# The first feed-forward product of a two-block kernel on one NeuronCore: two plain column blocks by token halves in four PSUM banks, the second block's weights split early

## The chip, the cores and the metric

The kernel runs on one NeuronCore of a Trainium2 chip. TensorE (PE) multiplies into PSUM, eight banks of 2 KB per partition; VectorE (DVE) and ScalarE (ACT) do elementwise work on SBUF and PSUM, GpSimd (POOL) on SBUF alone; SyncE (SP) and POOL issue the DMAs. Every engine works through its own instructions in the order in which they were written, and waits on semaphores. The metric is the device time of one execution in microseconds (us); lower is better.

## The reference

The program is two transformer-like blocks over 512 tokens of width 1024, in float32. The change lies at the end of the second block (D = 1024, D_FF = 4096), cut here to what matters:

```python
h = layer_norm(DEEPNORM_ALPHA * h + m @ w_out[l], ln1_g[l], ln1_b[l])
f = jnp.square(jax.nn.relu(h @ w_ff1[l])) @ w_ff2[l]
h = layer_norm(DEEPNORM_ALPHA * h + f, ln2_g[l], ln2_b[l])
```

## The kernel before, in words

**Products.** Every large product splits both operands into a high part (`fp32r`, an ACT copy: `split`, `up_hi_of`, `left_hi`, `right_hi`) and the rest (a DVE subtraction: `lower`), and issues three matmuls for each 128-row step: high x high, high x low, low x high (`three`, lines 456 to 458).

**Blocks.** `block_list` cuts the weights into blocks of 1 MB, numbered n. SP loads block n into `RAW[n % 2]`, ACT writes `WH`, DVE writes `WL`; there are two such pairs of slots and a third one (`WH[2]`, `WL[2]`), used by the two blocks of `OWN`, whose lower part POOL computes (`split_own`). DVE works for n: `split(n + 1)`, `side(n)`, `stage(n)` and `drain(n)`; ACT likewise. `W_OUT2` has four blocks, WO2 to WO2+3: the first two give columns 0 to 511 of `m @ w_out` (`tm_block`), the last two columns 512 to 1023 (`tm_pair`), each in banks 2 to 5, one bank for each 128-token tile. `stage` splits the left operand for the pair (ACT `x_hi`, DVE `x_lo`), and `drain(WO2+1)` adds the first two blocks' banks to the residual (`add_half`, four instructions on line 1765), which frees banks 2 to 5 for the pair.

**The layer norm rows.** The pair finishes one token tile after another. For each tile DVE adds (line 1765), takes statistics, centres (1788) and scales (1797), with a reciprocal root on POOL between; then PE transposes the row (`turn_row`, eight 128x128 transposes into banks 6 and 7, line 567), ACT writes the high part `TH` (line 1169) and a plain copy `H1T` (line 1170), and DVE subtracts into `TL` (`h1_rows_lo`). Rows 0 and 1 are turned within the pair, rows 2 and 3 within the next product.

**The first feed-forward product.** `h @ w_ff1` has 4096 columns in eight groups of 512. Group 0 is computed plainly, as two blocks of 256 columns (`ff1_0`, `ff1_0 + 1`), each in banks 0 and 1. The first goes through `fm_block_by_halves`: all of its work for tokens 0 to 255, during which rows 2 and 3 are turned, and then that for tokens 256 to 511, with 256-wide matmuls. The second goes through `fm_block` with 512-wide matmuls; it uses the same banks 0 and 1, so it waits until ACT has taken the first block out of them (`relus(0)`, line 1222). Its weights are loaded into `RAW[1]` and split after the rows.

**Groups 1 to 7** are computed by Winograd's form of Strassen's scheme, seven products a group (`ff1_multiply(q, i)`, order P1, P5, P6, P2, P7, P3, P4; 24 matmuls, 256 wide, in each; g counts them from 0 to 48). It wants sums of quadrants of `h` (`left_sums`, `left_sum_hi`, `left_sum_lo`), sums of quadrants of the weights (`up_sums`), and five rotating slots of split weights (`UPH`, `UPL`). Banks are combined by `part_copy` on ACT and `add_part` on DVE (line 1972): P6 waits for the copy of P1, P4 waits for `add_part` of P7. `difference` (1978) is work for the next product.

**The turn.** `ff @ w_ff2` follows in the same scheme: 28 products p of 24 matmuls, 512 wide. SP loads or POOL adds (an accumulating DMA) 1 MB of weights for each into one of four buffers `MRAW`, ACT makes `right_hi(p)` and `left_hi(p)`, DVE `right_lo(p)` and `left_lo(p)`, in three slots. The first of these stand among the last products of the first half, written out by hand in the loops `for g in range(FF1_PRODUCTS)` on both engines.

Of the kernel before, what the change touches and what calls it, by code (L numbers as in the profile page):

```python
# [49 lines left out]
def block_list(a):  # L50
# [42 lines left out]
    fm("ff1", w_ff1, 0, 512)  # L93
# [3 lines left out]
def two_blocks(nc, a, out, x1_spill, m_spill):  # L97
# [26 lines left out]
    def place(name, shape, dt=f32, size=4):  # L124
# [121 lines left out]

    H1T = at("h1_t", [P, KC, S], A + 56 * K1)
# [4 lines left out]
           enumerate((base + 16 * K1, base + 20 * K1, A + 80 * K1, base + 24 * K1, base + 28 * K1))]  # L252
    UPL = [at(f"w_ff1_lo{i}", [P, 4, 256], o, f32r) for i, o in
           enumerate((base + 32 * K1, base + 36 * K1, A + 84 * K1, base + 40 * K1, base + 44 * K1))]
# [6 lines left out]
    MRAW = RAW + [at(f"w_raw{i}", [P, 2048], TURNED + 8 * K1 * (i - 2)) for i in (2, 3)]  # L261
# [12 lines left out]
    with ctx:  # L274
# [13 lines left out]
        up_raw = [[sem(f"w_ff1_quadrant{k}{n}_loaded") for n in range(2)] for k in range(2)]  # L288
        up_sum, up_hi, up_lo = sem("w_ff1_sums"), sem("w_ff1_hi"), sem("w_ff1_lo")
# [74 lines left out]
        ff1_0, ff2_0 = first["ff1"], len(blocks)  # L364
# [75 lines left out]
        def _(pe):  # L440
# [34 lines left out]
            def fm_block_by_halves(n, name, done, turns):  # L475
# [4 lines left out]
                for half in range(2):  # L480
                    c = slice(half * S // 2, (half + 1) * S // 2)
                    for t in range(2):
# [452 lines left out]
            def product_ready(p):  # L935
                pe.wait_ge(w_lo, ff2_0 + p + 1)
# [18 lines left out]
        f0 = [turn["fm", ff1_0, t][1] for t in range(2)]  # L955
# [3 lines left out]
        def _(act):  # L959
# [99 lines left out]
            def side(n):  # L1059
# [39 lines left out]
                if 0 <= n - GO < TT:  # L1099
                    squares_o(n - GO)  # L1100
                    if n - GO + 2 < TT:
                        chunk_split(n - GO + 2)

            def drain(n):
# [59 lines left out]
                if name == "w_out2" and i == 3:  # L1164
                    for j in range(TT):
                        for half in range(2):
# [3 lines left out]
                            free(act.activation(H1T[:, c, tile_of(j)], quarters(b[:, :]), ACT.Copy), key)  # L1170
# [1165 lines left out]
```

## Time and profile before

| | |
|---|---|
| median of 3 runs | 1113.29 us (1112.86 to 1114.3) |
| the profiled execution's own time | 1111.89 us |
| its span in the trace | 1110.1 us |
| PE busy | 1081.9 us, 97% of the span |
| DVE, ACT, POOL busy | 706.2 us (64%), 496.1 us (45%), 90.7 us (8%) |
| mean granted clock of TensorE | 0.995 of full speed |

A row of the timeline has the start in us from the start of the span, the duration, engine, line, operation and tiles, a count, and in brackets the idle time before it with what ended it. Matmuls overlap, so the pace of a stream is the distance of its starts and not the duration shown.

### The profile page before, as it was taken

The page shows a single profiled execution, that of the slowest core. Times are in us where ns is not written, and L with a number is a line of the kernel's source. Part 1 is how long each engine was busy: PE and PEld are TensorE (multiplying, and loading weights), DVE is VectorE, ACT ScalarE, POOL GpSimd, SP SyncE. Part 2 cuts the span into 40 slices and gives each one's busy share as a digit, 9 for nine tenths or more (in the row PEclk, how much of TensorE's full clock was granted, in tenths as well). Part 3 has the DMA queues.
Part 4 walks back from the last instruction along what each step waited for, and adds up shares of the span by engine and source line. Part 5 has one row for each costly group of instructions (what it writes and reads, how often), then busy time and mean ns, then how long its engine had stood idle before and what let it go on. Part 6 is the DMA issues. An engine that isn't in the chain of part 4 may idle for free.

```text
span 1110.1 us, 13890 instructions
## 1 busy us (share of the span) xinstructions
PE 1081.9 (97%) x5812; PEld 929.7 (84%) x5812; DVE 706.2 (64%) x790; ACT 496.1 (45%) x566; POOL 90.7 (8%) x103
## 2 busy tenths in 40 slices
PE   8999999999999999999999999999899999999897
PEld 8788888888888888888888888888799999788685
DVE  5553356557355465547566555668777776998597
ACT  7444342443333442244433633343456666655451
POOL 3000000000012000001000010022000000221121
PEclk9999999999999999999999999999899999999999
DMA  8523322223232622223222222261142243999961
GB/s 281 192 79 114 124 69 75 86 76 114 76 111 80 208 76 93 97 76 96 76 76 76 76 76 77 76 220 47 39 150 78 95 135 115 216 205 246 280 208 57
DMA packets 91423, 131.75 MB, mean 119 GB/s; under 512 B 4797, under 2 KB 58429, under 8 KB 91233
## 3 DMA queue, kind: packets, MB, share of 16 engines
q1 hardware_dynamic: 79872, 103.19, 28.5%
q0 software_dynamic: 11200, 27.54, 11.1%
q8 instruction: 46, 0.75, 0.3%
q10 hardware_dynamic: 288, 0.13, 0.0%
q14 instruction: 17, 0.13, 0.0%
HBM read 126.65 MB, written 4.20 MB: 118 GB/s over the span
## 4 chain that ended last, share of the span: by engine, by line
PE 82%; DVE 8%; DMA 3%; ACT 3%; issue 2%; POOL 1%; POOLq 0%; DVEq 0%; SPq 0%; ACTq 0%
PE bank L456 25%; PE bank L458 24%; PE bank L457 24%; DMA w_raw<-in_w_ff 3%; PE bank L567 2%; DVE w_lo L1349 2%; PE bank L761 1%; DVE w_ff_lo L1349 1%; PE bank L687 1%; PE bank L668 1%; DVE bn L1653 1%; POOL rstd L2119 1%; PE bank L817 1%; PE bank L720 1%; PE bank L705 1%
## 5 line engine op out<-in xcount | busy, mean ns | idle before, releaser
L1349 DVE TENSOR_TENSOR w_lo<-w_raw,w_hi 128x2048 fp32r<-128x2048 f32 (+1 forms) x90 | 200.6, 2231 | 194.6 <-ACT w_hi L978 175.1
L456 PE MATMUL bank<-act_t_hi,w_hi 128*128 128x512 f32 (+1 forms) x608 | 234.3, 385 | 6.1 <-ACT ff_hidden L1222 3.6
L458 PE MATMUL bank<-act_t_hi,w_lo 128*128 128x512 f32 (+1 forms) x608 | 231.0, 380 | 0.0
L457 PE MATMUL bank<-act_t_lo,w_hi 128*128 128x512 f32 (+1 forms) x608 | 230.8, 380 | 0.0
L978 ACT ACTIVATE w_hi<-w_raw 128x2048 fp32r<-128x2048 f32 (+1 forms) x61 | 114.6, 1881 | 103.2 <-PE bank L458 95.0
L456 PEld LDWEIGHTS bank<-act_t_hi,w_hi 128*128 128x128 f32 x608 | 115.1, 189 | 28.0 <-issue 6.1
L458 PEld LDWEIGHTS bank<-act_t_hi,w_lo 128*128 128x128 f32 x608 | 114.9, 189 | 21.8
L457 PEld LDWEIGHTS bank<-act_t_lo,w_hi 128*128 128x128 f32 x608 | 115.1, 189 | 21.1 <-issue 0.2
L456 PE MATMUL bank<-w_hi,hidden_hi 128*128 128x512 f32 x224 | 87.6, 391 | 6.7 <-DVE w_lo L1349 6.1
L458 PE MATMUL bank<-w_hi,hidden_lo 128*128 128x512 f32 x224 | 87.2, 389 | 0.0
L457 PE MATMUL bank<-w_lo,hidden_hi 128*128 128x512 f32 x224 | 87.1, 389 | 0.0
L1349 DVE TENSOR_TENSOR w_ff_lo<-w_raw,w_ff_hi 128x1024 fp32r<-128x1024 f32 x49 | 59.9, 1223 | 31.7 <-ACT w_ff_hi L1236 31.7
L456 PE MATMUL bank<-w_hi,act_t_hi 128*128 128x512 f32 x192 | 75.8, 395 | 0.0
L458 PE MATMUL bank<-w_hi,act_t_lo 128*128 128x512 f32 x192 | 74.8, 390 | 0.0
L457 PE MATMUL bank<-w_lo,act_t_hi 128*128 128x512 f32 x192 | 74.7, 389 | 0.0
L1236 ACT ACTIVATE w_ff_hi<-w_raw 128x1024 fp32r<-128x1024 f32 x49 | 51.7, 1055 | 49.4 <-DVE w_raw L1955 19.9
L456 PE MATMUL bank<-act_t_hi,w_ff_hi 128*128 128x256 f32 x224 | 63.7, 284 | 2.8 <-DVE ff_hidden L1972 2.8
L457 PE MATMUL bank<-act_t_lo,w_ff_hi 128*128 128x256 f32 x224 | 63.4, 283 | 0.0
L458 PE MATMUL bank<-act_t_hi,w_ff_lo 128*128 128x256 f32 x224 | 63.4, 283 | 0.0
L456 PE MATMUL bank<-w_hi,x_hi 128*128 128x512 f32 x160 | 62.6, 391 | 0.0
L458 PE MATMUL bank<-w_hi,x_lo 128*128 128x512 f32 x160 | 62.3, 389 | 0.0
L457 PE MATMUL bank<-w_lo,x_hi 128*128 128x512 f32 x160 | 62.3, 389 | 0.0
(313 smaller groups left out, 1963.9 us busy)
## 6 DMA issues: line engine op xcount, KB each, us to landing
w_raw<-in_w_in SPq DMA_DIRECT2D x46, 1024.0 KB, 5.2
w_raw<-in_w_ff SPq DMA_DIRECT2D x18, 1024.0 KB, 5.7
w_raw<-in_w_ff POOLq DMA_DIRECT2D x16, 1024.0 KB, 10.9
w_raw<-in_w_ff SPq DMA_DIRECT2D x28, 512.0 KB, 4.3
w_raw<-in_w_out SPq DMA_DIRECT2D x10, 1024.0 KB, 5.2
w_raw<-in_w_mem_kv SPq DMA_DIRECT2D x3, 1024.0 KB, 7.2
residual<-in_x SPq DMA_DIRECT2D x4, 512.0 KB, 9.5
x_spill<-residual POOLq DMA_DIRECT2D x1, 2048.0 KB, 7.1
```

What stands on the lines that cost most here:

```text
L456: pe.matmul(dst, lh, rh, start=start, stop=False, skip_group_check=onto)
L457: pe.matmul(dst, lh, rl, start=False, stop=False, skip_group_check=onto)
L458: return pe.matmul(dst, ll, rh, start=False, stop=stop, skip_group_check=onto)
L567: last = pe.transpose(dst[:, tile_of(i)], src(i), IDENT[:, :])
L668: last = pe.matmul(bank[b][:, c0:c0 + S - i * P], QK[:, 4 + h, tile_of(i)], QK[:, h, i * P:S], start=True, stop=True)
L687: last = pe.matmul(dst[:, c:c + P + 1], PP[h % 2][:, w:w + P], V[:, i, h, :], start=i == 0, stop=i == j)
L705: last = pe.matmul(dst[:, q:q + NMEM], QC[:, h, tile_of(j)], KM[:, h, :], start=True, stop=True)
L720: last = pe.matmul(dst[:, tile_of(h)], VM[:, m, tile_of(h)], PT[j % 2][:, 2 * h + m, :], start=m == 0, stop=m == MT - 1)
L761: last = pe.matmul(dst[0:keys, i * P // 2:(i + 1) * P // 2], KE[:, c * P:c * P + keys], QEC[:, c * P // 2:(c + 1) * P // 2], start=True, s ...
L978: act.activation(WH[slot_of(n)][:, c0:w], RAW[n % 2][:, c0:w], ACT.Copy).then_inc(w_hi, 1)
L1236: act.activation(UPH[g % FF1_SLOTS][:, :, :], up_place(i), ACT.Copy).then_inc(up_hi, 1)
L1349: return dve.tensor_tensor(dst, src, hi.bitcast(f32), ALU.subtract)
```

## The change

- Both plain blocks of group 0 are one step, `ff1_pair_by_halves`: both blocks for tokens 0 to 255, then both for tokens 256 to 511, all in 256-wide matmuls, block 0 in banks 0 and 1, block 1 in banks 2 and 3. Row 2 is turned after k = 1 of the first tile, row 3 after k = 3 of the third tile.
- Block 1 is no longer a numbered block. SP loads it into a buffer of its own (`W2`) once m is ready, before the load of WO2+3; ACT and DVE split it in `side(WO2+1)`, ahead of the operand that `stage` splits for the pair.
- The first quadrants for group 1 are loaded and split earlier (`up_hi_of(0)` and `up_lo_of(0)` stand before row 3; `RAW[1]` is refilled before `RAW[0]`); the split slots are renumbered so that slots 0 to 3 only need the blocks of `w_out2` done. The lower part of row 3 is taken from PSUM, and its plain copy made after it.
- `relus(0)`, `relus(1)`, `squares(0)`, `squares(1)` and `difference` move to later places.
- At the turn, `right_hi(0)`, `left_hi(1)`, `right_hi(1)` on ACT and `left_lo(0)`, `right_lo(0)`, `left_lo(1)` on DVE stand before the end of the first half; `MRAW` is reordered so that the first weights can be loaded after product 44.

```diff
@@ block_list
-    fm("ff1", w_ff1, 0, 512)
+    fm("ff1", w_ff1, 0, 256)
@@ places
+    W2 = at("w_ff1_block1", [P, 2048], A + 80 * K1)
+    W2H = at("w_ff1_block1_hi", [P, 2048], A + 32 * K1, f32r)
+    W2L = at("w_ff1_block1_lo", [P, 2048], A + 80 * K1, f32r)
...
-           enumerate((base + 16 * K1, base + 20 * K1, A + 80 * K1, base + 24 * K1, base + 28 * K1))]
+           enumerate((base + 16 * K1, base + 20 * K1, base + 24 * K1, base + 28 * K1, A + 80 * K1))]
...
-    MRAW = RAW + [at(f"w_raw{i}", [P, 2048], TURNED + 8 * K1 * (i - 2)) for i in (2, 3)]
+    MRAW = [at("w_raw2", [P, 2048], TURNED), RAW[0], RAW[1], at("w_raw3", [P, 2048], TURNED + 8 * K1)]
@@ PE
-            fm_block_by_halves(ff1_0, "h1T", h1_done, {(0, 7): 2, (1, 5): 3})
-            fm_block(ff1_0 + 1, TH, TL)
+            def ff1_pair_by_halves(turns):
+
+                pair = weights(ff1_0, (WH, WL)), tuple(t[:, :].rearrange("p (k c) -> p k c", k=KC) for t in (W2H, W2L))
+                for half in range(2):
+                    c = slice(half * S // 2, (half + 1) * S // 2)
+                    for b, (wh, wlo) in enumerate(pair):
+                        if half == 0 and b == 0: pe.wait_ge(own_lo, 2)
+                        if half == 0 and b == 1: pe.wait_ge(w2_lo, 1)
+                        for t in range(2):
+                            key = ("fm", ff1_0 + b, t)
+                            if half == 0:
+                                take(2 * b + t, key)
+                            for k in range(KC):
+                                if b == 0 and t == 0 and k % 4 == 0:
+                                    for j in (2 * half, 2 * half + 1):
+                                        pe.wait_ge(h1_lo, 2 * j + k // 4 + 1)
+                                last = three(bank[2 * b + t][:, c], wh[:, k, tile_of(t)], wlo[:, k, tile_of(t)], TH[:, k, c], TL[:, k, c],
+                                             k == 0, k == KC - 1)
+                                if half == 0 and (b, t, k) in turns:
+                                    turn_row("h1T", h1_done, turns[b, t, k])
+                            if half:
+                                give(last, key)
...
+            ff1_pair_by_halves({(0, 0, 1): 2, (1, 0, 3): 3})
@@ ACT, side(n)
+                if n == WO2 + 1:
+                    act.wait_ge(w2_loaded, 16)
+                    act.activation(W2H[:, :], W2[:, :], ACT.Copy).then_inc(w2_hi, 1)
@@ ACT, up_hi_of(g)
-                elif g >= 3:
-                    act.wait_ge(*block_done[ff1_0 + 1])
+                else:
+                    act.wait_ge(*block_done[(WO2 + 2, WO2 + 2, WO2 + 3, WO2 + 3, ff1_0 + 1)[g]])
@@ ACT, left_hi(p)
-                if p == 1: act.wait_ge(ff1_product, FF1_PRODUCTS - 1)
+                if p == 1: act.wait_ge(ff1_product, FF1_PRODUCTS - 4)
@@ ACT, loop over g
+                if g == 1: relus(1)
                 if g == FF1_PRODUCTS - 4:
                     left_hi(0)
+                if g == FF1_PRODUCTS - 3:
+                    right_hi(0)
+                    left_hi(1)
                 if g == FF1_PRODUCTS - 2:
-                    right_hi(0)
+                    right_hi(1)
             relu_sum(PAIRS - 1, 2)
             square_last(PAIRS - 1)
-            right_hi(1)
             square_sum(PAIRS - 1, 2)
-            left_hi(1)
@@ DVE, side(n)
+                if n == WO2 + 1:
+                    dve.wait_ge(w2_hi, 1)
+                    lower(W2L[:, :], W2[:, :], W2H[:, :]).then_inc(w2_lo, 1)
@@ DVE, loop over g
-                if i == P6 and q % 2 == 0:
+                if i == P4 and q % 2 == 0:
                     difference(q // 2 - 1)
-                if g == FF1_PRODUCTS - 2:
+                if g == 2: squares(1)
+                if g == FF1_PRODUCTS - 3:
                     left_lo(0)
                     right_lo(0)
+                    left_lo(1)
+            right_lo(1)
+            difference(QUADS - 1)
             sum_two(0)
-            right_lo(1)
-            left_lo(1)
-            difference(QUADS - 1)
@@ SP
             for n in range(5, ff1_0):
+                if n == ff1_0 - 1:
+                    sp.wait_ge(m_ready, KC)
+                    sp.dma_start(W2[:, :].rearrange("p (k c) -> p k c", k=KC),
+                                 a["w_ff1_2"][0].rearrange("(k p) n -> p k n", p=P)[:, :, 256:512]).then_inc(w2_loaded, 16)
                 load(n, blocks[n][2])
...
-                if s < 2: sp.wait_ge(up_lo, FF1_PRODUCTS)
-                if s == 2: sp.wait_ge(ff1_product, FF1_PRODUCTS - 5)
+                if s == 0: sp.wait_ge(ff1_product, FF1_PRODUCTS - 5)
+                if s == 1: sp.wait_ge(up_lo, FF1_PRODUCTS)
```

How the order moves at three places. First DVE around the second half of `w_out2` (`w_lo` is a weight block's lower part, `x_lo` the left operand's, `w_ff_block` the new buffer `W2`), before and then now:

```order
L1349 TENSOR_TENSOR w_lo_53<-w_raw_49,w_hi_51 128x2048
L1349 TENSOR_TENSOR x_lo_84<-r_silu,x_hi_82 128x2048
L1349 TENSOR_TENSOR x_lo_89<-r_silu,x_hi_87 128x2048
L1765 SCALAR_TENSOR_TENSOR residual<-residual,bank 128x512 x4
L1349 TENSOR_TENSOR w_lo_54<-w_raw_50,w_hi_52 128x2048
```

```order
L1383 TENSOR_TENSOR w_lo_53<-w_raw_49,w_hi_51 128x2048
L1383 TENSOR_TENSOR w_ff_block_lo<-w_ff_block_158,w_ff_block_hi 128x2048
L1383 TENSOR_TENSOR x_lo_84<-r_silu,x_hi_82 128x2048
L1383 TENSOR_TENSOR x_lo_89<-r_silu,x_hi_87 128x2048
L1802 SCALAR_TENSOR_TENSOR residual<-residual,bank 128x512 x4
L1383 TENSOR_TENSOR w_lo_54<-w_raw_50,w_hi_52 128x2048
```

One 128x2048 subtraction now stands ahead of the four additions that free banks 2 to 5. Next the end of the first half on DVE (`hidden_lo` is `left_lo`, `w_lo` is `right_lo`, `ff_part` goes into `add_part`), before and now:

```order
L1972 TENSOR_TENSOR ff_hidden<-bank,ff_part_166 128x2x256
L1972 TENSOR_TENSOR ff_hidden<-bank,ff_part_167 128x2x256
L1349 TENSOR_TENSOR hidden_lo_188<-ff_hidden,hidden_hi_185 128x1024
L1349 TENSOR_TENSOR w_lo_53<-w_raw_49,w_hi_51 128x2048
L1984 TENSOR_TENSOR hidden_sum_178<-ff_hidden 128x1024
L1349 TENSOR_TENSOR w_lo_182<-w_raw_50,w_hi_181 128x2048
```

```order
L2015 TENSOR_TENSOR ff_hidden<-bank,ff_part_169 128x2x256
L1383 TENSOR_TENSOR hidden_lo_191<-ff_hidden,hidden_hi_188 128x1024
L1383 TENSOR_TENSOR w_lo_53<-w_raw_186,w_hi_51 128x2048
L1383 TENSOR_TENSOR hidden_lo_192<-ff_hidden,hidden_hi_189 128x1024
L2015 TENSOR_TENSOR ff_hidden<-bank,ff_part_170 128x2x256
L1383 TENSOR_TENSOR w_lo_185<-w_raw_49,w_hi_184 128x2048
```

The lower parts for product p = 0, and the left one for p = 1, now stand before the last `add_part`. Last ACT from row 3 on (`act_t_hi` is `TH`, `h_t` is `H1T`, `w_ff_hi` the split slots, L1222 is `relus`), before and now:

```order
L1169 ACTIVATE act_t_hi<-bank 128x4x128
L1170 ACTIVATE h_t<-bank 128x4x128
L978 ACTIVATE w_hi_52<-w_raw_50 128x2048
L1236 ACTIVATE w_ff_hi_168<-w_raw_49 128x1024
L1240 ACTIVATE h_sum_hi<-h_t 128x1024
L1222 ACTIVATE ff_hidden<-bank 128x512 x2
```

```order
L1144 ACTIVATE w_ff_hi_171<-w_raw_49 128x1024
L1213 ACTIVATE act_t_hi<-bank 128x4x128 x2
L1219 ACTIVATE h_t<-bank 128x4x128 x2
L1144 ACTIVATE w_ff_hi_172<-w_raw_50 128x1024
L1275 ACTIVATE h_sum_hi<-h_t 128x1024
L1144 ACTIVATE w_ff_hi_173<-w_raw_50 128x1024
```

The 128x2048 split of the second plain block has left this place, and the copies out of the banks (`relus`) come later.

## Rows read from the trace of the kernel before

**Rows 1.** The page's part 1, busy time, share of the span and instructions:

```profile
PE 1081.9 (97%) x5812; PEld 929.7 (84%) x5812; DVE 706.2 (64%) x790; ACT 496.1 (45%) x566; POOL 90.7 (8%) x103
```

**Rows 2.** Waits of PE, 716 to 1110 us: in total, times, longest:

```profile
PE bank L456 <- DVE w_lo L1349: 6.1, 3, 3.2
```

**Rows 3.** Timeline of PE, from the end of `w_out2` to product P1:

```profile
764.33 0.28 PE L456 MATMUL bank<-act_t_hi,w_hi 128*128 128x256 f32 x1
764.45 0.28 PE L457 MATMUL bank<-act_t_lo,w_hi 128*128 128x256 f32 x1
...
770.74 1.09 PE L567 MATMUL bank<-ident,residual 128*128 128x128 f32 x8 [0.36 <-DVE residual L1797]
...
773.46 0.36 PE L456 MATMUL bank<-act_t_hi,w_hi 128*128 128x256 f32 x1 [0.92 <-DVE act_t_lo L1349]
...
783.05 0.77 PE L456 MATMUL bank<-act_t_hi,w_hi 128*128 128x512 f32 x1 [3.60 <-ACT ff_hidden L1222]
...
796.58 0.28 PE L456 MATMUL bank<-act_t_hi,w_ff_hi 128*128 128x256 f32 x1
```

**Rows 4.** Windows: stretch, length, busy PE, PEld, DVE, ACT, POOL, clock, DMA, GB/s:

```profile
783.00:788.00 5.00, 4.95 (x12) 3.93 (x13) 5.00 (x6) 1.45 (x2) 0.00 (x0) 0.50 0.00 0
```

**Rows 5.** Timeline of DVE, second half of `w_out2` and row 2:

```profile
734.27 4.48 DVE L1349 TENSOR_TENSOR x_lo<-r_silu,x_hi 128x2048 fp32r<-128x2048 f32 x2
738.67 2.12 DVE L1765 SCALAR_TENSOR_TENSOR residual<-residual,bank 128x512 f32<-128x512 f32 x3
...
764.45 1.28 DVE L1797 SCALAR_TENSOR_TENSOR residual<-residual,rstd,ln_b_all 128x1024 f32<-128x1024 f32 x1
```

**Rows 6.** Timeline of PE, the pair's first matmul:

```profile
740.73 0.39 PE L456 MATMUL bank<-w_hi,x_hi 128*128 128x512 f32 x1
```

**Rows 7.** Timeline of POOL, the reload of the residual once m is ready:

```profile
722.06 0.81 POOL L2175 DMA_DIRECT2D residual<-x_spill  x1 [34.28 <-DVE r_silu L1649]
```

**Rows 8.** DMA issues, 715 to 760 us: count, size, median us to landing:

```profile
w_raw<-in_w_out SPq DMA_DIRECT2D x1, 1024.0 KB, 11.6
```

**Rows 9.** Timeline of DVE, between P1 and P4 of group 1:

```profile
797.87 1.23 DVE L1349 TENSOR_TENSOR act_t_lo<-h_t,act_t_hi 128x1024 fp32r<-128x1024 f32 x1 [3.57 <-ACT act_t_hi L1240]
799.01 1.22 DVE L1349 TENSOR_TENSOR w_ff_lo<-w_raw,w_ff_hi 128x1024 fp32r<-128x1024 f32 x1
...
802.49 1.23 DVE L1349 TENSOR_TENSOR w_ff_lo<-w_raw,w_ff_hi 128x1024 fp32r<-128x1024 f32 x1 [1.12 <-ACT w_ff_hi L1236]
...
816.00 0.68 DVE L1972 TENSOR_TENSOR ff_hidden<-bank,ff_part 128x512 f32<-128x512 f32 x1
```

**Rows 10.** Timeline of PE, waits in groups 1 to 7 and at the turn:

```profile
803.09 0.36 PE L456 MATMUL bank<-h_sum_hi,w_ff_hi 128*128 128x256 f32 x1 [0.60 <-ACT ff_part L1273]
...
816.83 0.36 PE L456 MATMUL bank<-act_t_hi,w_ff_hi 128*128 128x256 f32 x1 [1.93 <-DVE ff_hidden L1972]
...
837.49 0.35 PE L456 MATMUL bank<-act_t_hi,w_ff_hi 128*128 128x256 f32 x1 [0.28 <-DVE ff_hidden L1972]
...
942.10 0.28 PE L458 MATMUL bank<-act_t_hi,w_ff_lo 128*128 128x256 f32 x1
943.62 0.50 PE L456 MATMUL bank<-w_hi,hidden_hi 128*128 128x512 f32 x1 [1.24 <-DVE w_lo L1349]
...
949.98 0.47 PE L456 MATMUL bank<-w_hi,hidden_hi 128*128 128x512 f32 x1 [0.62 <-DVE hidden_lo L1349]
```

**Rows 11.** Timeline of ACT, then of DVE, at the turn, weights of p = 0:

```profile
937.92 1.90 ACT L1253 ACTIVATE w_hi<-w_raw 128x2048 fp32r<-128x2048 f32 x1
...
941.28 2.29 DVE L1349 TENSOR_TENSOR w_lo<-w_raw,w_hi 128x2048 fp32r<-128x2048 f32 x1
```

**Rows 12.** Windows of the second product, columns as in group 4:

```profile
950.00:1005.00 55.00, 55.00 (x243) 45.53 (x244) 52.59 (x40) 29.45 (x22) 13.37 (x11) 1.00 1.13 204
...
1044.00:1048.00 4.00, 2.02 (x9) 1.67 (x10) 3.75 (x3) 0.55 (x1) 0.00 (x0) 1.00 1.08 292
```

**Rows 13.** Timeline of PE, its longest wait in the second product:

```profile
1045.98 0.50 PE L456 MATMUL bank<-w_hi,hidden_hi 128*128 128x512 f32 x1 [3.24 <-DVE w_lo L1349]
```

More of the change, by code:

```diff
@@ L362, in tile_of @@
             return slice(j * P, j * P + P)
-        ff1_0, ff2_0 = first["ff1"], len(blocks)
+        ff1_0 = first["ff1"]
+        HI_0, LO_0 = len(blocks), len(blocks) - 1
         assert ff1_0 % 2 == 0
@@ L935, in product_ready @@
             def product_ready(p):
-                pe.wait_ge(w_lo, ff2_0 + p + 1)
+                pe.wait_ge(w_lo, LO_0 + p + 1)
                 pe.wait_ge(x_lo, E_FF2 + p + 1)
@@ L1169, in drain @@
                             act.activation(TH[:, c, tile_of(j)], quarters(b[:, :]), ACT.Copy).then_inc(h1_hi, 1)
-                            free(act.activation(H1T[:, c, tile_of(j)], quarters(b[:, :]), ACT.Copy), key)
+                            if j < TT - 1:
+                                free(act.activation(H1T[:, c, tile_of(j)], quarters(b[:, :]), ACT.Copy), key)
+                    for half in range(2):
+                        key, c = ("h1T", TT - 1, half), slice(4 * half, 4 * half + 4)
+                        act.wait_ge(h1_lo, 2 * TT - 1 + half)
+                        free(act.activation(H1T[:, c, tile_of(TT - 1)], quarters(bank[6 + half][:, :]), ACT.Copy), key)
             def stage(n):
@@ L1293, in square_last @@
                 act.activation(f, f, ACT.Square).then_inc(f1_done, 1)
-            split(ff1_0 + 1)
-            up_hi_of(0)
+            up_hi_of(1)
             left_sum_hi(SAH[0][:, :, :], turned(H1T, 0, 0), 3)
-            relus(0)
-            up_hi_of(1)
             up_hi_of(2)
@@ L1778, in h1_rows_lo @@
                     dve.wait_ge(h1_hi, 2 * j + half + 1)
-                    drained(dve, ("h1T", j, half))
-                    lower(TL[:, c, tile_of(j)], H1T[:, c, tile_of(j)], TH[:, c, tile_of(j)]).then_inc(h1_lo, 1)
+                    if j == TT - 1:
+                        src = quarters(bank[6 + half][:, :])
+                    else:
+                        drained(dve, ("h1T", j, half))
+                        src = H1T[:, c, tile_of(j)]
+                    lower(TL[:, c, tile_of(j)], src, TH[:, c, tile_of(j)]).then_inc(h1_lo, 1)
             def center_rows(n0, j, g, v):
@@ L1930, in left_sums @@
                 a11, a12, a21, a22 = (turned(H1T, m, k) for m in range(2) for k in range(2))
-                dve.wait_ge(h1_lo, 2 * TT)
+                for half in range(2):
+                    drained(dve, ("h1T", TT - 1, half))
                 dve.tensor_tensor(a22, a21, a22, ALU.add).then_inc(left_sum, 1)
@@ L2041, in last_norm @@
                                              ALU.add).then_inc(h2_done, 1)
-            split(ff1_0 + 1)
+            up_sums(1)
             left_sums()
-            up_lo_of(0)
-            left_sum_lo(SAL[0][:, :, :], turned(H1T, 0, 0), SAH[0][:, :, :], 1)
-            up_sums(1)
-            squares(0)
             up_lo_of(1)
             up_sums(2)
+            left_sum_lo(SAL[0][:, :, :], turned(H1T, 0, 0), SAH[0][:, :, :], 1)
             up_lo_of(2)
@@ L2241, in _ @@
                     thin_load(a["w_in_2"], 5 * D)
-            for n in range(2):
-                load(ff1_0 + n, blocks[ff1_0 + n][2])
+            load(ff1_0, blocks[ff1_0][2])
             def load_up(q, k, n):
@@ L2249, in _ @@
                 if q == 1:
+                    sp.wait_ge(w_lo, LO_0)
+                    load_up(q, 0, 1)
+                    load_up(q, 1, 1)
                     sp.wait_ge(own_lo, 2)
```

101 lines of the change are left out of this document (50 added, 51 removed).

## Prediction

> **What bounds the kernel now.** PE does. Read the page's busy times first: PE is busy 97% of the span [rows 1], so a change can only gain PE's idle time, matmuls that run slowly, or matmuls left out. Then PE's waits and its timeline: the reader is to see that the idle time after 716 us stands at four places: the head of the feed-forward part [rows 3], the first product group and the even ones after it, the turn to the second product (both [rows 10]), and one stretch of the second product [rows 13]. Waits for `w_lo` alone are 6.1 us of it [rows 2]. The costliest place is the head: PE stops 0.36 and 0.92 us for row 3, then 3.60 us for `relus(0)` to free bank 0 [rows 3], and comes back at half clock: granted 0.50 from 783 to 788 us, the lower level of 1.2 GHz, with 12 matmuls in 5 us [rows 4], where the full level gives 22 (0.227 us each, 55.00 us for 243 [rows 12]). The sum is made against the profiled execution (1111.89 us, span 1110.1); the median shown is 1.4 us above that.
>
> **The change, part by part.**
>
> *Narrower matmuls.* Starts of 256-wide matmuls lie 0.12 us apart [rows 3], so two cost 0.24 where one of 512 costs 0.227. The second block's 48 become 96: 0.6 us lost, contained in the stream below. The Trainium skill, "TensorE: Matmul & The Clock Gate", section "Back-to-back issue gap", gives columns over 2.4 GHz plus 2.5 ns. By it (an estimate) the edit would cost 0.1 us and the sum would be 0.5 us better; the rows decide.
>
> *The new split on DVE and ACT.* DVE's two `x_lo` start at 734.27 and the first `add_half` at 738.67, done at 739.4 [rows 5]; PE's pair starts at 740.73 and needs its bank 2 [rows 6]. Now a 128x2048 subtraction stands ahead, which moves what follows by 2.2 (4.4 for two [rows 5]): bank 2 is free at 741.6, and with 0.15 us from DVE's end to PE's start (816.68 to 816.83 [rows 9, 10]) and a slower first matmul PE loses **1.1 us**. The layer norm rows wait for the pair's results and shift by the same. This holds if `W2` has landed when ACT reaches it, one subtraction before 734.27, at 732. Its load may go out once m is ready, at 722 [rows 7]. The trace has no such load; the nearest is the 1 MB for WO2+3 in the same stretch, 11.6 us to landing [rows 8], which gives 733.6, ACT 1.6 late and PE some 2.3 in all. The other end is 0, if DVE's order is made up for before 740. I take 1.1, since `W2` is first in SP's queue and the 1 MB of rows 8 was behind 3 MB of POOL's. The Trainium skill, "DMA: Bandwidth & Descriptors", section "Queues, rings and completion order", says that a DMA engine takes turns between queues, packet by packet. By that the load keeps half the rate beside the reload of the residual and is there before 732, the sum stays; if they were served in order of issue, it would be the 2.3.
>
> *The head's stream.* Before, 764.33 to 796.58 is 32.25 us [rows 3]. Now it starts at 765.4. A turn costs 0.9 (740.73 to 764.33 is 23.6 us [rows 3, 6], less 96 x 0.227, for two). Row 2's scale ends at 765.73 [rows 5], now 766.8; PE is there after six matmuls, at 766.1, and waits 0.7. Row 3 stands 54 matmuls later, at 774.2, when it has long been ready; its first lower half took 2.7 us from the turn (770.74 to 773.46 [rows 3]), so 776.9, and is needed at 779.5: no wait, and none for banks, of which there are four. So 1.1 + 0.7 + 192 x 0.12 + 1.8 = 26.6, and P1 starts at 791.0: **5.6 us gained**. With no stop over 1.1 us the clock should keep its upper level, as it did after 3.24 [rows 12, 13].
>
> *From P1 to P4 of group 1.* Before 20.25 us (796.58 to 816.83 [rows 3, 10]) against 6 x 24 x 0.12 = 17.3, so 3.0 lost, of it 0.60 for ACT's copy and 1.93 for `add_part`. Unhindered P4 would now start at 808.3. DVE idled 3.57 us until the plain blocks ended [rows 9]; now it has work without a break from 776.9: 24 operations 1.14 apart (797.87 to 799.01 [rows 9]) and one of 0.6 before `add_part` of P7, with three waits of up to 1.1 for ACT's copy of a fresh sum, as at 802.49 [rows 9]. That is 808.3, done at 809.0 (0.68). P4 still waits 0.8: **2.1 gained**. Bounds: 0.8 more without those waits, 1.3 less with the full old one. P6's copy is first in ACT's queue now, `relus(1)` behind it.
>
> *Groups 2 to 7.* From 816.83 to the end of product 49 at 942.22 [rows 10] are 125.4 us against 43 x 2.88 = 123.8. The 1.5 lost are three stops like that at 837.49 [rows 10], where `difference` delays `add_part`; it moves behind P4: **1.5 gained**, or nothing if another subtraction is late in its place.
>
> *The turn.* Let T be the end of product 49. The weights of p = 0 now load after product 44 (T - 14.4); their copy starts after product 47 (T - 5.8), 1.90, then the subtraction, 2.29 [rows 11]: ready at T - 1.6. Before, 942.22 to 943.62 went by: **1.4 gained**. Queued behind it, the last `add_part` slips to T - 0.4 and `right_hi(1)` waits for that; p = 1 is ready at T + 4.4 and used at T + 5.4. So 943.62 to 949.98, 6.36 us [rows 10], becomes 24 x 0.227 = 5.45: **0.9 gained**. Late next is p = 2, ready at T + 10.6, due at T + 10.9.
>
> *The second product.* Its DMAs are nearly without pause (share 1.13 [rows 12]), but progress of PE and DVE releases them, so they move along; the 3.24 us before 1045.98 stays [rows 13]. SP issues one load more before that of WO2+3, which has to wait for an earlier split anyway; POOL's queue is the same. The split that left the head, the renumbered slots and the moved squares lie within the DVE count above.
>
> **Sum:** 5.6 + 2.1 + 1.5 + 1.4 + 0.9 = 11.5 us. 1111.89 - 11.5 = 1100.4; from the median shown, **1101.8 us**.
>
> **Rivals.**
> 1. *Only the head pays.* DVE becomes the bound: P4, the even groups and the turn keep their waits. For it: DVE has 32 us of unbroken work, and the margins at the turn are 0.3 and 1.0 us. Against: DVE still idles in every group. 5.6 to 7 us, about 1107.
> 2. *The clock falls elsewhere.* The stop of 3.24 us ended at full clock, that of 3.60 at half [rows 3, 4, 12, 13]. If the first becomes slightly longer, or merely falls otherwise, 12 matmuls take 0.42 instead of 0.227: 2.4 us back, 1104.2. The Trainium skill's page on TensorE, section "HAM oscillation", tells of waits on DMAs that put the engine back to half clock; the stop at 783 agrees, the one at 1046 does not.
> 3. *Slower: ACT stands behind `W2`.* Its copy is ahead of both `x_hi`. From a landing at 732 on, each us late moves `x_hi`, `x_lo`, the drains of the banks and PE by one; with 2.4 us for the clock this eats the 11.5 from a landing at 741, 19 us after issue, and at 744 gives 1116. The nearest load took 11.6 [rows 8], so it is unlikely.
> 4. *It does not do what it says:* the long stop only moves, to row 3 or to the second half, 3.6 us and half clock again. Within 0.2% of before.
>
> **How the numbers follow.** Forecast 0.62 (1099 to 1104), rival 1 0.18, rival 2 0.12, rival 3 0.04, rival 4 0.04. Low end: P4 without a wait, no stall at bank 2: 11.5 + 1.9 = 13.4, 1099.9, and 0.9 below for the waits of the second product; the high end takes in rivals 1 and 2. Two in 25 are left out. A measurement can tell some 0.2% (2.2 us) from no change: faster 0.92, same 0.04, slower 0.04.
>
> **What would show it.** PE's timeline: a stop of 1 us near 741, one of 0.7 near 766, none near 783, clock 1.00 there; P1 at 791, P4 waiting under 1 us at 809; no stops of 0.28 in even groups; p = 0 right behind product 49, near 933. Wrong would be: over 2 us near 741 (rival 3), P4 past 811 or waits on `w_lo` for p = 0 to 2 (rival 1), a granted clock of 0.50 anywhere after 716 (rival 2 or 4).

## The result, and the profile after

The changed kernel takes 1107.28 us (median of 4 runs, 1106.17 to 1108.30), the kernel before in the same rounds 1113.50 (1112.86 to 1114.30): a ratio of 0.9945, 95% interval 0.993 to 0.996. Run once more beside later experiments it came to 1107.30 us, ratio 0.9939 (0.9925 to 0.9952). So it is faster, by 6.2 us, where the forecast was 11.5 us and a range of 1099.0 to 1107.0: **the forecast gain was nearly twice the measured one**. The median lies 0.3 us above the range, less than the runs differ among themselves, so which side of its end it falls on is chance. The missing 5 us of gain are not.

The profiled execution took 1108.3 us, span 1106.5, the slowest of the four; the one of before [rows 1], at 1111.89 us, was faster than all four runs of that kernel. Its busy times, part 1 of the page, answer to [rows 1]:

```profile
PE 1084.9 (98%) x5860; PEld 934.5 (84%) x5860; DVE 705.6 (64%) x790; ACT 497.2 (45%) x566; POOL 91.5 (8%) x103
```

Its timeline of PE: first the landmarks (start of `w_out2`, of the stop for bank 2, of the turned rows, P1, P4 of group 1, p = 0), then every stop behind P4 of group 1 up to the last product. Number in brackets: the idle time before the row.

```profile
721.40 0.39 PE L461 MATMUL bank<-w_hi,x_hi 128*128 128x512 f32 x1
...
744.13 0.47 PE L461 MATMUL bank<-w_hi,x_hi 128*128 128x512 f32 x1 [0.81 <-DVE residual L1802]
...
757.83 0.63 PE L569 MATMUL bank<-ident,residual 128*128 128x128 f32 x4
...
769.28 0.99 PE L569 MATMUL bank<-ident,residual 128*128 128x128 f32 x7 [0.58 <-DVE residual L1838]
...
793.39 0.28 PE L461 MATMUL bank<-act_t_hi,w_ff_hi 128*128 128x256 f32 x1
...
811.42 0.36 PE L461 MATMUL bank<-act_t_hi,w_ff_hi 128*128 128x256 f32 x1 [0.59 <-DVE ff_hidden L2015]
...
935.27 0.40 PE L461 MATMUL bank<-w_hi,hidden_hi 128*128 128x512 f32 x1
...
1025.39 0.79 PE L461 MATMUL bank<-w_hi,hidden_hi 128*128 128x512 f32 x1 [2.78 <-DVE w_lo L1383]
...
1040.14 0.50 PE L461 MATMUL bank<-w_hi,hidden_hi 128*128 128x512 f32 x1 [0.73 <-DVE w_lo L1383]
...
1048.16 0.50 PE L461 MATMUL bank<-w_hi,hidden_hi 128*128 128x512 f32 x1 [2.29 <-DVE w_lo L1383]
```

Read it against [rows 3, 10, 13]. The stop of 3.60 us is gone, so are the 0.28 of the even groups and both stops at the turn; P4 waits 0.59 where it waited 1.93. But the second product, which had 3.24 and 1.58 us of stops from 1000 us on (the second at 1053.33), now has 2.78, 0.73 and 2.29, and two of them end at half clock, which the windows show (columns as in [rows 4]):

```profile
1025.00:1031.00 6.00, 5.61 (x13) 4.45 (x14) 3.30 (x4) 2.64 (x2) 1.28 (x1) 0.50 1.11 246
...
1048.00:1052.00 4.00, 3.84 (x10) 3.01 (x11) 3.96 (x4) 3.28 (x3) 0.00 (x0) 0.58 0.77 238
```

**A trap first.** From profile to profile only 3.6 us of span are gained. 2.4 us of the rest arose ahead of the change: `w_out2` begins at 721.40, before at 718.97. In this execution the clock fell at 542 us, behind a stop of 1.29 us in code that is the same in both kernels; that is 1.6 us of the 2.4, and 0.8 stood there already. So distances are taken between landmarks, each read from the same row of both timelines:

| stretch | before | changed | gained | forecast |
|---|---|---|---|---|
| start of `w_out2` to the first turned row | 35.36 | 36.43 | -1.1 | -1.1 |
| to P1 | 42.25 | 35.56 | 6.7 | 6.7 |
| P1 to p = 0 | 147.04 | 141.88 | 5.2 | 5.0 |
| p = 0 to the last matmul | 158.37 | 163.14 | **-4.8** | 0.9 |

(The rows of before are at 718.97, 754.33, 796.58, 943.62 and 1101.99. "The last matmul" is the last but one on record, the same in every profile. A few records are missing from any trace, so each is good to 0.2 us.) Three of four lines are right within 0.2 us. All that is wrong is wrong in the second product. The line "to P1" owes something to the profile that it is read against: in the profiles of experiments 4 and 8 below the kernel before takes 41.29 and 41.27 us to P1, not 42.25, since its clock is half for 2.6 and 3.1 us there and not for 4.8. Against those the head gains 1 us less.

**Where it went.** There PE waits for `w_lo`, DVE's split waits for ACT's copy, and ACT's copy for DMAs. The view of waits from 930 to 1060 us, of the kernel before and then of the changed one:

```profile
POOL w_raw L2186 <- DMA w_raw<-in_w_ff: 29.3, 4, 12.2
ACT w_hi L1253 <- DMA w_raw<-in_w_ff: 15.7, 3, 7.2
```

```profile
ACT w_hi L1288 <- DMA w_raw<-in_w_ff: 43.3, 16, 7.3
POOL w_raw L2227 <- DMA w_raw<-in_w_ff: 43.3, 5, 17.3
```

Before, 3 of ACT's 28 copies waited for a DMA, now 16 do. (The count tells that the stream is late, and not how long PE stops: in experiments 1, 2, 6 and 10 below it is 3 to 5 again, with 4.3 to 6.1 us of stops.) Four tiles `w_raw0` to `w_raw3` hold the quarters of the second product's weights; each product's weights come by a plain load of 1 MB (SP's queue), by an accumulating DMA of 1 MB onto what lies there (POOL's), or by both. The windows of the changed kernel show the DMA engines' busy share and rate in the last two columns (a share of 1.0 or more is how engines without a pause read here):

```profile
932.00:936.00 4.00, 4.00 (x33) 3.87 (x32) 3.75 (x3) 1.83 (x4) 1.36 (x1) 1.00 0.02 7
936.00:946.00 10.00, 10.00 (x46) 8.23 (x44) 7.94 (x6) 8.03 (x9) 0.00 (x0) 1.00 0.94 211
946.00:949.00 3.00, 3.00 (x14) 2.37 (x13) 3.00 (x4) 2.73 (x2) 2.21 (x2) 1.00 0.06 8
949.00:1000.00 51.00, 51.00 (x226) 42.23 (x225) 47.37 (x37) 28.75 (x20) 11.90 (x10) 1.00 1.12 203
```

The engines stand idle from 932 to 936 us and from 946 to 949, and then run at 203 GB/s without pause. At that rate an accumulating DMA of 1 MB takes 5.2 us (1.05 MB over 203 GB/s, an estimate), and a product of PE 5.44. So a late stream gains 0.2 to 0.3 us a product on PE, some 2 us up to 1000 us. Then come the products p = 16 to 19, whose weights need a plain load and an accumulating DMA on top of it: an estimated 2.6 + 5.2 us of stream for 5.44 of PE. There the stream falls behind, and there the stops are (1025.39 is p = 16, 1040.14 and 1048.16 are p = 18 and 19). POOL's timeline tells of the second gap:

```profile
934.33 1.36 POOL L2227 DMA_DIRECT2D w_raw<-in_w_ff  x1 [161.53 <-DVE w_lo L1383]
946.79 2.59 POOL L2227 DMA_DIRECT2D w_raw<-in_w_ff  x2 [11.10 <-DMA w_raw<-in_w_ff]
```

After its first accumulating DMA POOL waits for the quarters s = 2 and 3 to be loaded (`for s in (2, 3): pool.wait_ge(quad_raw[s], 16)`). The load of s = 3 goes to a tile that product 49 reads, so it is issued only at 935.47, behind the accumulating DMA of 934.33 instead of ahead of it. Before, the order was the other way round. The view of DMA issues of before, then after (size, us to landing):

```profile
w_raw<-in_w_ff SPq DMA_DIRECT2D x1, 1024.0 KB, 5.0
w_raw<-in_w_ff POOLq DMA_DIRECT2D x1, 1024.0 KB, 8.5
```

```profile
w_raw<-in_w_ff POOLq DMA_DIRECT2D x1, 1024.0 KB, 11.6
w_raw<-in_w_ff SPq DMA_DIRECT2D x1, 1024.0 KB, 10.8
```

Beside each other both take about 11 us, and POOL's second issue waits for the later of them, which lands at 946.3. From that issue at 946.79 to its first bytes, at 948.7 in windows of half a microsecond, another 1.9 us go by; behind the issue at 934.33 it was some 2.1. In experiment 1 below, where POOL issues at 939.49, no such pause shows. The Trainium skill, "DMA: Bandwidth & Descriptors", section "Queues, rings and completion order", has a DMA engine take turns between queues; by that the plain load has to share, and the trace agrees: 10.8 us, where it took 5.0 ahead of the other.

**Theory A**, for the experiments: the stream of DMAs bounds the second product, and its start is tied to the end of product 49, where the load of s = 3 may go, and to POOL's wait. **Theory B**: the late stops come of DVE, ACT or the clock. **Theory C**: POOL's wait is worth its price, since it keeps the load of s = 3 fast.

### The profile page after: what moved, and what is told of

Its sections match the earlier page's. It is cut to its first block, busy times and chain, and to the rows that moved or that the text cites. A ratio compares the mean times of both kernels' runs of the same rounds, so it can differ in the third digit from the quotient of the medians.

```text
span 1106.5 us, 13986 instructions
## 1 busy us (share of the span) xinstructions
PE 1084.9 (98%) x5860; PEld 934.5 (84%) x5860; DVE 705.6 (64%) x790; ACT 497.2 (45%) x566; POOL 91.5 (8%) x103
## 4 chain that ended last, share of the span: by engine, by line
PE 79%; DVE 8%; DMA 7%; ACT 2%; issue 2%; POOL 1%; POOLq 0%; DVEq 0%; SPq 0%; ACTq 0%
PE bank L461 23%; PE bank L463 23%; PE bank L462 23%; DMA w_raw<-in_w_ff 6%; DVE w_lo L1383 2%; PE bank L569 2%; PE bank L763 1%; PE bank L689 1%; PE bank L670 1%; DVE bn L1687 1%; POOL rstd L2160 1%; PE bank L819 1%; PE bank L722 1%; PE bank L707 1%; DVE hidden_lo L1383 1%
## 5 line engine op out<-in xcount | busy, mean ns | idle before, releaser
L461 PE MATMUL bank<-act_t_hi,w_hi 128*128 128x512 f32 (+1 forms) x592 | 227.3, 384 | 1.6 <-ACT u_gelu L1197 1.3
L463 PE MATMUL bank<-act_t_hi,w_lo 128*128 128x512 f32 (+1 forms) x592 | 224.5, 379 | 0.0
L462 PE MATMUL bank<-act_t_lo,w_hi 128*128 128x512 f32 (+1 forms) x592 | 224.3, 379 | 0.0
L461 PEld LDWEIGHTS bank<-act_t_hi,w_hi 128*128 128x128 f32 x592 | 111.8, 189 | 22.6 <-issue 2.3
L463 PEld LDWEIGHTS bank<-act_t_hi,w_lo 128*128 128x128 f32 x592 | 111.8, 189 | 21.2
L462 PEld LDWEIGHTS bank<-act_t_lo,w_hi 128*128 128x128 f32 x592 | 111.8, 189 | 20.4 <-issue 0.2
L1288 ACT ACTIVATE w_hi<-w_raw 128x2048 fp32r<-128x2048 f32 x28 | 53.5, 1912 | 47.1 <-DMA w_raw<-in_w_ff 43.3
```

The lines of the kernel that those rows point to most:

```text
L461: pe.matmul(dst, lh, rh, start=start, stop=False, skip_group_check=onto)
L462: pe.matmul(dst, lh, rl, start=False, stop=False, skip_group_check=onto)
L463: return pe.matmul(dst, ll, rh, start=False, stop=stop, skip_group_check=onto)
L1288: act.activation(MH[p % 3][:, :], MRAW[s][:, :], ACT.Copy).then_inc(w_hi, 1)
```

## Experiments

### 1. No wait on POOL

```diff
             add_block(M1, 0, 0, 1)
-            for s in (2, 3):
-                pool.wait_ge(quad_raw[s], 16)
             for s in range(1, QUADS): add_block(M1, s, 0, 1)
```

The wait for data is kept by each `add_block`'s own wait on the split of its quarter.

> The changed kernel, where POOL no longer waits for the fourth quarter of the second product's weights before its second accumulating DMA. Theory A (the stream of DMAs bounds the second product; the changed kernel leaves the DMA engines idle from 945.7 to 948.7 us for this wait): the stream starts some 3 us earlier, so the waits of PE on w_lo shrink by about as much: 1104 to 1105 us. Theory B (PE waits there for DVE and ACT, or the lost 5 us are the clock's alone): no change, 1107. Theory C (the wait keeps the accumulating DMAs from the load of the fourth quarter, and is worth its price): that load lands later, a stop before the fourth product, 1108 or more.

Measured: 1103.68 us (1103.04 to 1106.16), ratio to before 0.9916 (0.9903 to 0.9930): 3.6 us less than the changed kernel. Its second accumulating DMA goes out at 939.49, and the gap is gone:

```profile
946.00:949.00 3.00, 3.00 (x15) 2.46 (x14) 2.52 (x3) 3.00 (x3) 0.72 (x1) 1.00 1.13 208
```

PE's stops behind 1000 us are 1.79, 0.76, 1.31 and 2.25 us, all ending at full clock. From p = 0 to the last matmul are 159.29 us, of 163.14. This fits theory A and not B, and it is the opposite of C: two deleted lines are worth more than half of what the whole change brought.

### 2. The old turn

The order of the tiles, `SP`'s waits, and ACT's and DVE's order around product 49 as in the kernel before:

```diff
-    MRAW = [at("w_raw2", [P, 2048], TURNED), RAW[0], RAW[1], at("w_raw3", [P, 2048], TURNED + 8 * K1)]
+    MRAW = RAW + [at(f"w_raw{i}", [P, 2048], TURNED + 8 * K1 * (i - 2)) for i in (2, 3)]
...
-                if g == FF1_PRODUCTS - 3:
+                if g == FF1_PRODUCTS - 2:
                     left_lo(0)
                     right_lo(0)
-                    left_lo(1)
```

> The changed kernel with the turn to the second product as it was before (order of the quarters in their tiles, their loads, ACT's and DVE's order); head and groups stay changed. Theory A: PE reaches the second product 2.3 us later, as the sum on record says, and gets it back from the stops on w_lo, since the DMA stream starts with all four quarters loaded: 1106.5 to 1108 us, within 1 us of the changed kernel. Theory B (the gain of the turn stays): 2.3 us more than the changed kernel, 1109.5.

Measured: 1105.09 us (1102.86 to 1105.69), ratio 0.9921 (0.9908 to 0.9935): 2.2 us *less* than the changed kernel, which none of the theories had. (The intervals touch; all six runs of this kernel are below eight of the nine of the changed one.) PE is 1.4 us later at p = 0 and stops 0.63 us at p = 1, as it did before. But POOL's wait costs nothing here, its second accumulating DMA being released by DVE's split:

```profile
934.97 1.36 POOL L2226 DMA_DIRECT2D w_raw<-in_w_ff  x1 [164.13 <-DVE w_lo L1382]
940.39 1.29 POOL L2226 DMA_DIRECT2D w_raw<-in_w_ff  x1 [4.05 <-DVE w_lo L1382]
```

So the new turn, alone, makes the kernel slower: it lets PE begin 1.4 us earlier on a stream that begins 3 us later. Theory A's number missed, since the expectation had left POOL's wait out; its mechanism fits.

### 3 and 4. Plain loads in place of the accumulating DMAs

In the changed kernel (3) and in the kernel before (4), all 16. The sums of quarters are left out, so both compute with other weights:

```diff
-                pool.dma_start(four_chunks(MRAW[s]), down[s, k, n], accum_op=ALU.add).then_inc(quad_sum[s], 16)
+                pool.dma_start(four_chunks(MRAW[s]), down[s, k, n]).then_inc(quad_sum[s], 16)
```

> The changed kernel, with the 16 accumulating DMAs of the second product turned into plain loads of the same size (the output is then that of other weights). Theory A: at twice the rate the DMA engines no longer bound the second product, all of PE's stops on w_lo after 1000 us go, with the half clock behind two of them: 1099 to 1101 us, 6 to 8 less than the changed kernel. Theory B: the stops stay, for they come from DVE and ACT: 1106 to 1107.

> The same edit in the kernel before. Theory A: it loses its two stops of 3.24 and 1.58 us and comes to 1108.5 to 1110; the distance to the changed kernel with the same edit is then 9.5 to 11.5 us, near the forecast sum of 11.5, where it was 6.2. Theory B: the distance stays at 6.

Measured: 1096.61 us (1095.16 to 1097.12), ratio 0.9845, and 1106.84 us (1106.10 to 1108.32), ratio 0.9941, both against the same runs of before. Both are some 2 us faster than theory A's numbers. 10.2 us lie between them, as A had it, where 6.2 lay with the accumulating DMAs, and the forecast sum was 11.5; 1 us of what is still missing may be the head of the kernel before, 41.29 us to P1 in this profile. Neither has a stop of PE in the second product but the one for p = 1 of before (0.60 us). From p = 0 to the last matmul they take 151.97 and 152.91 us: with a faster stream the change gains the 0.9 us in the second product that the forecast gave it. In (3) the engines are even idle between products, and the view of waits has no row at all of ACT waiting for a DMA:

```profile
955.00:957.00 2.00, 2.00 (x11) 1.65 (x10) 2.00 (x3) 0.45 (x1) 0.75 (x1) 1.00 0.00 0
```

The stops do not come of DVE, ACT or the clock: theory B is out for them.

### 5. The changed kernel once more

> The changed kernel once more, beside the runs that follow. Theory A (stream of DMAs): 1107.3 as before; however the clock falls in the stretch from 1000 to 1050 us, idle time and slow matmuls of PE in it come to some 10 us, since the stream ends when it ends. Theory B (the half clock there was chance and is what it lost): some runs 4 us faster, and a profile without half clock there shows 6 us lost.

Measured: 1107.30 us (1105.14 to 1108.34), ratio 0.9939 (0.9925 to 0.9952). Its profile has other stops and another clock than the first one, 4.60, 1.67 and 2.28 us, and only the first ends at half clock:

```profile
1026.77 0.50 PE L461 MATMUL bank<-w_hi,hidden_hi 128*128 128x512 f32 x1 [4.60 <-DVE w_lo L1383]
...
1049.28 0.50 PE L461 MATMUL bank<-w_hi,hidden_hi 128*128 128x512 f32 x1 [2.28 <-DVE w_lo L1383]
```

From p = 0 to the last matmul it takes 163.06 us, of 163.14, but so close a match is luck. PE leaves its last stop 1.5 us later after P1 than in the first profile (256.3 and 254.8), and then needs 1.6 us less, since here the clock is full behind it and there it was half. What speaks for theory A is the table at the end: half clock *ahead* of the last stop does not make it later.

### 6. The fourth quarter loaded early

Beside experiment 1's edit, `w_raw3` moves to where a sum of tokens' halves lay, which is free after product 47, and the hidden sums (now four tiles `S2[s]`) and two vectors of the last layer norm move in exchange; two of the sums wait one product longer. Cut:

```diff
-    MRAW = [at("w_raw2", [P, 2048], TURNED), RAW[0], RAW[1], at("w_raw3", [P, 2048], TURNED + 8 * K1)]
+    MRAW = [at("w_raw2", [P, 2048], TURNED), RAW[0], RAW[1], at("w_raw3", [P, 2048], XS + 16 * K1)]
...
-                if s == 3: sp.wait_ge(ff1_product, FF1_PRODUCTS)
+                if s == 3: sp.wait_ge(ff1_product, FF1_PRODUCTS - 2)
```

> The changed kernel without POOL's wait, and with the fourth quarter of the weights loaded three products earlier (its tile lies where the sums of the tokens' halves lay, which are free sooner; two of the hidden sums take its old place). Theory A: the DMA engines no longer stand from 932 to 936 us before that load and POOL's first accumulating DMA, the stream is 2.6 us (1 MB at 400 GB/s) shorter from there, and so is the kernel: 1101 to 1102 us. Theory B (nothing hangs on the stream's start): as without POOL's wait alone, 1103.7 to 1104.

Measured: 1102.64 us (1101.88 to 1103.10), ratio 0.9898 (0.9883 to 0.9913). That is 1.0 us better than experiment 1 by the medians, with intervals that overlap, not 2.6. The load no longer runs beside the accumulating DMA, which lands in 8.3 us instead of 11.5. But now the stream pauses for want of something to do, as here, where the split of the next quarter releases it:

```profile
941.00:943.00 2.00, 2.00 (x10) 1.65 (x10) 2.00 (x3) 2.00 (x2) 0.00 (x0) 1.00 0.82 103
...
1004.00:1008.00 4.00, 4.00 (x20) 3.30 (x19) 3.96 (x4) 2.57 (x2) 2.44 (x2) 1.00 0.73 153
```

That is less than half of A's number, and in experiment 11, the same kernel again, nothing is left of it. It looks as if the stream's start had stopped being the limit.

### 7. The second plain block's subtraction later

Experiment 6, with DVE's split of `W2` moved from its side work in `w_out2` to behind `half_stats`, where DVE had idled 1.81 us.

> The same, and DVE's subtraction for the second plain block behind the statistics of the rows, where DVE waited 1.81 us for PE. Theory A: PE's stop of 0.81 us at 744 goes, and since it stands ahead of the stream, it pays in full: 0.8 us less than the kernel before it, 1100.3 to 1101.2. Theory B (the stream eats this too, or the layer norm rows come late): no change or 0.5 slower.

Measured: 1105.79 us (1103.48 to 1107.64), ratio 0.9928 (0.9914 to 0.9943), 3 us slower than experiment 6, where theory B had up to 0.5. The stop at 744 goes, but the subtraction takes 4.32 us in its new place, of DVE's timeline, and the layer norm's rows come late: PE waits for the first of them and goes on at half clock, 0.68 of full speed over 757 to 761 us.

```profile
747.98 4.32 DVE L1383 TENSOR_TENSOR w_ff_block_lo<-w_ff_block,w_ff_block_hi 128x2048 fp32r<-128x2048 f32 x1
```

```profile
757.34 1.09 PE L569 MATMUL bank<-ident,residual 128*128 128x128 f32 x8 [2.19 <-DVE residual L1835]
```

POOL's own subtraction runs from 745.17 to 750.15 there; from its end to DVE's are 2.15 us, about one subtraction of DVE alone (2.28). The Trainium skill, "SBUF — State Buffer", section "SBUF: two separate sides", has DVE with two inputs in SBUF and POOL take turns at one pair of ports, an instruction at a time; the trace agrees.

### 8. Control: no wait on POOL in the kernel before

> The kernel before without POOL's wait for its third and fourth quarters: a control. Theory A: no change, 1113.5, since its second accumulating DMA at 949.29 us was released by DVE's split, when both quarters had landed. Theory C (the wait costs wherever it stands): 3 us faster.

The same two lines are deleted. Measured: 1113.91 us (1112.00 to 1114.39), ratio 0.9997 (0.9988 to 1.0007). The wait costs nothing there. It is the pair, the new turn and the old wait, that costs.

### 9 and 11. The second plain block's split earlier, and experiment 6 again

Experiment 6, with copy and subtraction of `W2` ahead of the split for which both engines idle at 731 us:

```diff
             for n in range(ff1_0):
+                if n == WO2 + 1:
+                    act.wait_ge(w2_loaded, 16)
+                    act.activation(W2H[:, :], W2[:, :], ACT.Copy).then_inc(w2_hi, 1)
                 split(n + 1)
```

and the same for DVE.

> The kernel with the fourth quarter loaded early and without POOL's wait, and with the copy and the subtraction for the second plain block ahead of the split that both ACT (idle for 6.40 us) and DVE (5.86 us) wait for at 731 us; its load has landed at 728.8. Theory A (what stands ahead of the stream pays in full): the stop of 0.81 us goes, the rows are 1.1 us earlier, 1101.5 where the kernel without this edit has 1102.6. Theory B: no change.

> The kernel with the fourth quarter loaded early once more, beside the one with the second plain block's split moved: 1102.6 as before under either theory; it fixes the distance of the other to it.

Measured: 1104.23 us (1103.99 to 1104.53), ratio 0.9912 (0.9898 to 0.9927), beside 1103.67 us (1102.76 to 1104.65), ratio 0.9907 (0.9893 to 0.9922). By the times, nothing gained. In the trace the 1.1 us are there: no stop at 744, 35.36 us from `w_out2` to the first row where it was 36.43, and PE leaves its last stop 323.02 us after the start of `w_out2`, in experiments 6 and 11 after 323.96 and 324.20. But in this profile the clock is half behind the last stop, where no wait is left to hide it:

```profile
1042.00:1048.00 6.00, 5.39 (x13) 4.24 (x14) 5.96 (x6) 3.72 (x3) 0.00 (x0) 0.50 0.80 237
```

That costs 2.8 us (51.49 from there to the last matmul instead of 48.64); in the profile of experiment 11 it is half for a shorter while, 49.97 us. Whether the edit pays over many executions is left open; the intervals cannot tell.

### 10. One accumulating DMA less

The changed kernel, its first accumulating DMA a plain load.

> The changed kernel, with POOL's wait, and with only the first of the 16 accumulating DMAs a plain load (the output is then that of other weights for one quarter). Theory A: the stream is 2.5 us shorter at its very start (1 MB at 400 instead of 205 GB/s), 80 us ahead of the stops, and the kernel by as much: 1104.8. Theory B (the late stops come of the dense stretch from 1000 us on, where plain and accumulating loads stand one behind the other): no change, 1107.3.

Measured: 1103.48 us (1102.96 to 1105.62), ratio 0.9911 (0.9894 to 0.9927), 3.8 us less. An edit at 934 us takes its whole price out of stops 90 us later, as it must if the stream is what PE waits for there; theory B had no change. The transfer itself is an estimated 2.5 us shorter; the rest is that s = 3 no longer shares with a slow one, so that POOL's wait ends earlier and the stream runs from 945 us, of 949:

```profile
941.00:945.00 4.00, 4.00 (x20) 3.30 (x19) 4.00 (x3) 4.00 (x3) 1.34 (x1) 1.00 0.16 27
945.00:1003.00 58.00, 58.00 (x257) 47.90 (x256) 53.07 (x41) 31.63 (x23) 12.79 (x10) 1.00 1.12 208
```

### Together

Times after P1 in each profile. The second accumulating DMA starts to move when the first has landed (its issue plus its time to landing) or, with a gap, when the windows show bytes again:

| kernel | second accumulating DMA moves | PE leaves its last stop | last matmul |
|---|---|---|---|
| before | 155.8 | 256.8 | 305.4 |
| changed | 155.3 | 254.8 | 305.0 |
| changed, once more (5) | 155.4 | 256.3 | 305.0 |
| no wait on POOL (1) | 152.4 | 252.5 | 301.2 |
| old turn (2) | 151.9 | 253.0 | 303.3 |
| first one plain (10) | 151.9 | 252.1 | 300.8 |
| before, no wait on POOL (8) | 157.7 | 258.3 | 306.9 |
| fourth quarter early (6) | 149.3 | 252.0 | 300.7 |
| the same again (11) | 149.5 | 252.2 | 302.2 |
| the same, `W2` split earlier (9) | 149.1 | 252.1 | 303.6 |

PE leaves its last stop 99.5 to 101.1 us after the stream gets going, whoever waits for whom at the turn. Experiment 8 is a test by chance: its clock fell behind the stop at 817.90 us, the turn came 1.8 us later after P1 than in the profile of before, and the last stop 1.5 us later. Half clock ahead of the last stop does not lengthen the distance: it is 99.5, 100.9 and 100.6 where the clock was half for 2.6 to 5.7 us there (changed, 5, 8) and 100.1 to 101.1 where it was full (before, 1, 2, 10). Matmuls at half clock there only fill a wait.

Only in the last three lines, where the stream starts at 149, does something else hold at 252. What it is, no run here shows. One thing to look at is the change from accumulating DMAs to plain loads, where the stream does pause: at 1004 to 1008 us in experiment 6, and in the kernel before down to a share of 0.31 at 1014.5 us.

Before and after the change the stream starts at the same time after P1. Product 49 ends 3.8 us earlier (141.9 us after P1 instead of 145.6), the first accumulating DMA lands 0.5 us later behind it (10.7 us instead of 10.2), and POOL's gap is 2.8 us: 0.5 us are left. **Nearly everything that the change gains behind P1, 5.2 us at p = 0, is given back; what is left is the head.** From the last stop on it is 48.6 us at full clock, and 50.2 where it is half for a while (the changed kernel and experiment 2).

## Why the prediction was wrong

- *Narrower matmuls, the split ahead of the pair, bank 2:* right. PE loses 1.1 us; its stop at 744.13 is 0.81, and `W2` landed 5.5 us after its issue, where the nearest row had 11.6 [rows 8]. It was hardly slowed by the reload of the residual beside it (a plain load of 1 MB took 5.0 at the turn), so this row does not tell taking turns from serving in order of issue.
- *The head's stream:* right. 5.6 us net, row 2 turned after a stop of 0.58 (forecast 0.7), no stop at 783, clock 1.00 up to the stop at 1025, P1 35.56 us after the first turned row (42.25 before).
- *P1 to P4, even groups, turn:* right as far as PE is followed to p = 0: 5.2 us for 5.0 forecast, P4 waiting 0.59 (0.8), no stops of 0.28, p = 0 right behind product 49.
- *The second product:* this is the step that failed. It said of the DMAs there that "progress of PE and DVE releases them, so they move along". The share of 1.13 [rows 12] was in hand and was read as a remark. If DMA engines are without pause for 50 us and PE then stops for weights, it is they that release PE, and not PE them, and then the question is what starts them. That is the end of product 49 for the load of s = 3, and POOL's wait on it. The sentence "POOL's queue is the same" was true of its order; what it waits for had moved behind another transfer. The term was put at 0, beside the 0.9 gained for p = 1 that was counted at the turn. The stretch measured -4.8 for +0.9: 5.7 us, of the 11.5.
- *Rival 1* gave the right time, 1107, by luck and with the wrong cause: P4, the even groups and the turn did not keep their waits, and DVE is not the bound. Its likeness, only the head pays, holds for the reason above. *Rival 2* came true in a form of its own: the clock fell behind two stops in this profile. Ahead of the last stop that cost nothing that the table shows, behind it 1.6 us (50.2 for 48.6). What the rival takes from the Trainium skill is told there of waits on DMAs; the stop at 783 was one for ACT, so only the half clock behind it agrees. Rivals 3 and 4 did not happen.
- *The chances:* a rival for the DMA stream was missing, and with it a loss in the second product as the other bound of that step. 0.92 for faster was right.

The fastest version that still computes the product is experiment 6 (1102.64 and 1103.67 us, 0.9898 and 0.9907 of before). Deleting POOL's wait alone gives 0.9916, and the rest is within the intervals.

## What to carry to other kernels

A DMA share that stays above 1 over a long stretch, with the compute engine stopping for its data at the end of it, is the sign that the stretch is as long as its transfers: ask what starts that stream, not when the compute engine gets there, and count every gain ahead of it only up to that point. A wait that costs nothing in one order of transfers can cost 3 us in another, so re-read each wait on a queue whose neighbours you move; when PE arrives early at a saturated stream, its gain reappears as stops far behind, here 90 us later. And compare stretches between landmarks, not spans: two executions differed by 2.4 us before they reached the change.

## What the runs showed of the hardware that I had not expected

- *The clock falls by no rule of length that I can see.* Behind stops of 2.28 and 2.29 us at the same place of the same kernel it was full once (5) and half once (the first profile). It was full behind 3.24 us [rows 13], 2.94 (2) and 2.25 (1), half behind 3.60 [rows 3, 4], 4.60 (5), 3.01 (11), 2.23 (6) and, in unchanged code at 542 us, behind 1.29; there before it was full behind 1.28. The Trainium skill, "TensorE: Matmul & The Clock Gate", section "HAM oscillation", tells of waits on DMAs that halve the clock. Some of these stops do so, and nothing here says which.
- *An accumulating DMA runs at half the rate of a plain one:* about 205 GB/s against about 405, for the same bytes written, with the engines busy all the time in both (shares of 1.1 and 1.05). Mixed, plain and accumulating, they ran at about 262, near the 272 that equal bytes of both would give one after the other.
- *An accumulating DMA of POOL moves its first bytes 1.8 to 2.1 us after its issue* (934.33 and 946.79 us in the changed kernel, 942.45 in experiment 10).
- *DVE's subtraction of 2.28 us took 4.32* beside one of POOL (experiment 7).
